# Residual and product blocks moved by DMA into the place of the low part, and transposed from there as fp32r

## What is computed

```python
# first block
h = rmsnorm(x, norm_attn);  q, k, v = split(h @ w_in)        # 8 dilated heads, 8 differential heads
x = x + concat(ya, yb) @ w_out                               # out_a, out_b
h = rmsnorm(x, norm_ffn)
x = x + (silu(h @ w_gate) * (h @ w_up)) @ w_down             # ffn1, inner width 5632
x = rmsnorm(x, norm_final)
# second block
z = rmsnorm(x) @ w_in2                                       # in_m, in_f, gate_m, gate_a
merged = g_a * (a_out @ w_proj_a) + g_m * (m_out @ w_proj_m) # proj_a ends this sum
x = x + merged @ w_out2                                      # out2
u = causal_dwconv(rmsnorm(x) @ w_up2)                        # ffn2
x = x + (silu(u_gate) * u_val) @ w_down2
```

## Time and profile before

| | us |
|---|---|
| median of 3 runs (2583.82 to 2584.75) | 2584.1 |
| profiled execution, its own time | 2584.64 |
| profiled execution, span of the instructions | 2582.8 |
| PE busy | 2562.9 (99% of the span) |
| weight loads of PE (beside its matmuls) | 2280.2 (88%) |
| DVE busy | 1453.2 (56%) |
| ACT busy | 1224.1 (47%) |
| DMA engines, mean busy share | 58%, 182 GB/s |

### The profile page before, as it was taken

One profiled execution on the slowest core, in us unless ns is written; L12 is line 12 of the kernel. 1 busy time (PEld: TensorE's weight loads), 2 busy tenths in 40 slices (PEclk: granted clock), 3 DMA queues, 4 the chain that ended last, 5 costly groups with the idle time before them and its releaser, 6 DMA issues.

```text
span 2582.8 us, 40276 instructions
## 1 busy us (share of the span) xinstructions
PE 2562.9 (99%) x14246; PEld 2280.2 (88%) x14246; DVE 1453.2 (56%) x1743; ACT 1224.1 (47%) x1677; POOL 104.4 (4%) x171
## 2 busy tenths in 40 slices
PE   8999999999999999999999999999999999999999
PEld 8999988888888888888899888788999899998997
DVE  5555555555555555555455545465576646765674
ACT  5665545444344434455455544544454434543443
POOL 1111100000000000000000000100000000000000
PEclk9999999999999999999999999999999999999999
DMA  7555556665665566666555655555555555555554
GB/s 214 155 159 162 168 183 186 189 188 192 193 191 187 189 194 191 191 196 188 166 168 170 187 170 172 163 171 185 176 181 184 195 189 185 181 188 194 173 191 165
DMA packets 328631, 469.37 MB, mean 182 GB/s; under 512 B 21911, under 2 KB 137810, under 8 KB 328402
## 3 DMA queue, kind: packets, MB, share of 16 engines
q1 hardware_dynamic: 328530, 468.04, 58.1%
HBM read 465.87 MB, written 2.10 MB: 181 GB/s over the span
## 4 chain that ended last, share of the span: by engine, by line
PE 84%; issue 14%; POOL 1%; SPq 0%; DMA 0%; DVE 0%; ACT 0%; POOLq 0%; DVEq 0%; ACTq 0%
PE ps L429 20%; PE ps L431 20%; PE ps L430 20%; PE ps L443 7%; PE ps L442 7%; PE ps L441 7%; PE ps L498 1%; PE ps L645 1%; PE ps L676 0%; PE ps L549 0%; POOL head_rstd L1844 0%; PE ps L480 0%; PE ps L486 0%; PE ps L568 0%; SPq L328 0%
## 5 line engine op out<-in xcount | busy, mean ns | idle before, releaser
L1276 DVE TENSOR_TENSOR w_lo<-raw,w_hi 128x1024 fp32r<-128x1024 f32 (+1 forms) x928 | 1095.3, 1185 | 1080.3 <-ACT w_hi L879 1079.0
L879 ACT ACTIVATE w_hi<-raw 128x1024 fp32r<-128x1024 f32 (+1 forms) x928 | 947.7, 1025 | 1151.0 <-PE ps L431 961.6
L429 PE MATMUL ps<-w_hi,xT_hi 128*128 128x512 f32 (+1 forms) x2400 | 906.8, 378 | 2.9 <-DVE w_lo L1276 2.8
L431 PE MATMUL ps<-w_hi,xT_lo 128*128 128x512 f32 (+1 forms) x2400 | 893.6, 372 | 0.0
L430 PE MATMUL ps<-w_lo,xT_hi 128*128 128x512 f32 (+1 forms) x2400 | 892.9, 372 | 0.0
L429 PEld LDWEIGHTS ps<-w_hi,xT_hi 128*128 128x128 f32 x2400 | 451.5, 188 | 69.4 <-issue 6.6
L431 PEld LDWEIGHTS ps<-w_hi,xT_lo 128*128 128x128 f32 x2400 | 451.1, 188 | 64.3
L430 PEld LDWEIGHTS ps<-w_lo,xT_hi 128*128 128x128 f32 x2400 | 451.7, 188 | 62.4
L441 PE MATMUL ps<-yT_hi,w_hi 128*128 128x256 f32 x1408 | 398.6, 283 | 0.0
L443 PE MATMUL ps<-yT_hi,w_lo 128*128 128x256 f32 x1408 | 398.5, 283 | 0.0
L442 PE MATMUL ps<-yT_lo,w_hi 128*128 128x256 f32 x1408 | 398.5, 283 | 0.0
(11 more groups left out here) (191 smaller groups left out, 994.4 us busy)
## 6 DMA issues: line engine op xcount, KB each, us to landing
raw<-in_w_up SPq DMA_DIRECT2D x264, 512.0 KB, 3.6
raw<-in_w_down SPq DMA_DIRECT2D x176, 512.0 KB, 4.4
raw<-in_w_in SPq DMA_DIRECT2D x112, 512.0 KB, 3.7
raw<-in_w_in SPq DMA_DIRECT2D x256, 192.0 KB, 2.6
raw<-in_w_gate SPq DMA_DIRECT2D x88, 512.0 KB, 3.5
raw<-in_w_out SPq DMA_DIRECT2D x60, 512.0 KB, 4.1
raw<-in_w_in SPq DMA_DIRECT2D x64, 384.0 KB, 3.3
raw<-in_w_proj_m SPq DMA_DIRECT2D x16, 512.0 KB, 3.5
```

The lines of the kernel that those rows point to most:

```text
L429: pe.matmul(o, hi[:, q], w_hi[n % NS][:, k, 0:width], start=first, stop=False)
L431: mm = pe.matmul(o, lo[:, q], w_hi[n % NS][:, k, 0:width], start=False, stop=last)
L879: nc.scalar.activation(w_hi[n % NS][:, :, 0:width], raw[n % NS][:, :, 0:width], ACT.Copy).then_inc(hi_ready, 1)
L1276: v.tensor_tensor(w_lo[n % NS][:, :, 0:width], raw[n % NS][:, :, 0:width], f32(w_hi[n % NS][:, :, 0:width]), ALU.subtract).then_inc(lo_rea ...
```

## The change

A semaphore and two steps come between DVE's result and PE's transposes. SP gets `move_x` and `move_act`: a DMA from `fresh` or `tok_act` to that part of `xT_lo` or `yT_lo` in which the low part of the same tiles will stand (ffn2's input is in `yT_lo`). A quarter of the residual goes in two DMAs of 256 KB, one for each tile of 128 tokens as soon as its addition is done, in rows of 256 words; the product goes in one DMA of 512 KB. The words are moved as they are, as float32. `turn_x` and `turn_act` now wait for the DMA (`x_moved`, `act_moved`), read from the destination, which has the type fp32r, and use an identity in fp32r (`ident_r`, one copy on ACT). They hang behind unit 2 instead of 1 (and `units + 2`), and so do `x_hi`, `x_lo` and, with them, `sum_squares`; `hi_part` and `lo_part` stay behind unit 2. To place the moves, SP's loops of the stages concerned are written out. `move_x` hangs behind the load of unit `(q + 1) * units + 7`, `move_act` behind that of unit 7 of the next block.

```diff
+        ident_r = sb("ident_r", [P], F32R)
...
+        def quarter(v, c0):
+            return v[:, c0:c0 + NT * W].rearrange("p (t n) -> p t n", t=NT)
...
+            def move_x(q, base, summed=None):
+
+                sem_, c0 = summed or (by_dve, FREE + SUMMED[base])
+                dst = (yT_lo if base == 4 * KT else xT_lo)[:, q * NT * W:(q + 1) * NT * W].bitcast(F32)
+                for t in range(NT):
+                    sp.wait_ge(sem_, c0 + 2 * q + t + 1)
+                    sp.dma_start(dst.rearrange("p (b t n) -> p b t n", b=2, t=NT)[:, :, t, :],
+                                 fresh[q % 2][:, t, :].rearrange("p (b n) -> p b n", b=2)).then_inc(x_moved[q % 2], 16)
+
+            def moving(units, base, summed=None):
+
+
+                def in_stage(u):
+                    for q in range(4):
+                        if u == (q + 1) * units + 7:
+                            move_x(q, base, summed)
+                return in_stage, lambda u: in_stage(4 * units + u)
+
+            def move_act(up, i):
+
+                sp.wait_ge(by_dve, at(i, FREE + PH[up][BY_DVE], 4))
+                dst = yT_lo[:, 12 * S:16 * S].bitcast(F32)
+                sp.dma_start(dst.rearrange("p (t n) -> p t n", t=NT), tok_act).then_inc(act_moved, 16)
...
+                if u > 16 and u % 16 == 7:
+                    move_act(f"ffn1_up{t}", u // 16)
...
-            def turn_x(q, base, summed=None):
-
-
-                sem_, c0 = summed or (by_dve, FREE + SUMMED[base])
-                pe.wait_ge(sem_, c0 + 2 * q + 2)
+            def turn_x(q, base):
+
+
+                pe.wait_ge(x_moved[q % 2], 32 * (2 * (base // KT - 1) + q // 2 + 1))
                 pe.wait_ge(kt_lo, base + 4 * q - 4)
+                moved = quarter(yT_lo if base == 4 * KT else xT_lo, q * NT * W).rearrange("p t n -> p (t n)")
+                moved = moved.rearrange("p (b t n) -> p b t n", b=2, t=NT)
                 for b in range(2):
                     for c in range(2):
                         for t in range(NT):
                             kt = 2 * b + c
-                            mm = pe.transpose(ps[4 + 2 * (q % 2) + b][:, c * S + t * P:c * S + (t + 1) * P],
-                                              fresh[q % 2][:, t, kt * P:(kt + 1) * P], ident[:])
+                            out_ = ps[4 + 2 * (q % 2) + b][:, c * S + t * P:c * S + (t + 1) * P]
+                            mm = pe.transpose(out_.bitcast(F32R), moved[:, b, t, c * P:(c + 1) * P], ident_r[:])
                     mm.then_inc(kt_T, 1)
...
-            def turn_act(up, fg, i):
-
-                pe.wait_ge(by_dve, at(i, FREE + PH[up][BY_DVE], 4))
+            def turn_act(fg, i):
+
+                pe.wait_ge(act_moved, at(i, 16 * (fg + 1), 16))
                 pe.wait_ge(tok_lo, at(i, FREE + 2 * fg, 2))
+                moved = quarter(yT_lo, 12 * S)
                 for f in range(4):
                     for t in range(NT):
-                        mm = pe.transpose(ps[4 + f // 2][:, f % 2 * S + t * P:f % 2 * S + (t + 1) * P],
-                                          tok_act[:, t, f * P:(f + 1) * P], ident[:])
+                        out_ = ps[4 + f // 2][:, f % 2 * S + t * P:f % 2 * S + (t + 1) * P]
+                        mm = pe.transpose(out_.bitcast(F32R), moved[:, t, f * P:(f + 1) * P], ident_r[:])
                 mm.then_inc(tok_T, 1)
...
             act.wait_ge(gain_ready, 3)
+            nc.scalar.activation(ident_r[:], ident[:], ACT.Copy).then_inc(warm, 1)
...
-                        if u == 1 and i == 1:
+                        if u == 2 and i == 1:
                             x_hi(1, base, dst, gain0)
-                        if u == units + 1:
+                        if u == units + 2:
                             x_hi(2 * i, base, dst, gain0)
```

More of the change, by code:

```diff
@@ L272, in two_blocks @@
         x2_ready, warm = sem("x2_ready"), sem("warm")
+        x_moved, act_moved = [sem(f"x_moved{j}") for j in range(2)], sem("act_moved")
         stored = sem("stored")
@@ L332, in heads_turn, with stream, turn @@
                             behind(8 * g + u)
-            def stream(name, loops, parts):
+            def stream(name, loops, parts, behind=None):
                 step = sum(len(units) for units, _, _ in parts)
-                with sp.Fori(0, loops) as i:
+                def turn(i, then=None):
                     n = PH[name][0]
@@ L344, in stream, with pairs @@
                             load(n, i, step, src, width)
+                            if then:
+                                then(n - PH[name][0])
                             n += 1
-            def pairs(name, loops, units, c0, width):
-                stream(name, loops, [(units, lambda i, g=g: i * (2 * width) + (c0 + g * width), width) for g in range(2)])
+                if behind:
+                    for i in range(loops):
+                        turn(i, lambda u, i=i: behind(i * step + u))
+                else:
+                    with sp.Fori(0, loops) as i:
+                        turn(i)
+            def pairs(name, loops, units, c0, width, behind=None):
+                stream(name, loops, [(units, lambda i, g=g: i * (2 * width) + (c0 + g * width), width) for g in range(2)], behind)
+            def move_x(q, base, summed=None):
[15 more added lines that the diff above has]
+                sp.dma_start(dst.rearrange("p (t n) -> p t n", t=NT), tok_act).then_inc(act_moved, 16)
             w_in, w_out, w_in2 = a["w_in"][0], a["w_out"][0], a["w_in_2"][0]
@@ L389, in _ @@
                         load(n, i, 8, src[:, :, c:c + W], W)
-            pairs("out_a", 2, rows(w_out, 0, HALF), 0, W)
+            own, after_out_a = moving(4, KT)
+            pairs("out_a", 2, rows(w_out, 0, HALF), 0, W, own)
             with nc.allow_non_contiguous_dma("a few gate columns"):
@@ L410, in _, with at_out2 @@
             pairs("gate_a", 2, rows(w_in2), OFF_GA, W)
-            pairs("proj_a", 2, rows(a["w_proj_a_2"][0]), 0, W)
-            pairs("out2", 2, rows(a["w_out_2"][0]), 0, W)
-            ffn("ffn2", a["w_up_2"][0], a["w_up_2"][0], FF, a["w_down_2"][0])
+            own, after_proj = moving(4, 3 * KT, (fresh_ready, 0))
+            pairs("proj_a", 2, rows(a["w_proj_a_2"][0]), 0, W, own)
+            own, after_out2 = moving(8, 4 * KT)
+            def at_out2(u):
+                after_proj(u)
+                own(u)
+            pairs("out2", 2, rows(a["w_out_2"][0]), 0, W, at_out2)
+            ffn("ffn2", a["w_up_2"][0], a["w_up_2"][0], FF, a["w_down_2"][0], lambda t, u: after_out2(u) if t == 0 else None)
             out_v = out[0].rearrange("(t p) n -> p t n", p=P)
@@ L644, in turn_x, with residual @@
                             kt = 2 * b + c
-                            mm = pe.transpose(ps[4 + 2 * (q % 2) + b][:, c * S + t * P:c * S + (t + 1) * P],
-                                              fresh[q % 2][:, t, kt * P:(kt + 1) * P], ident[:])
+                            out_ = ps[4 + 2 * (q % 2) + b][:, c * S + t * P:c * S + (t + 1) * P]
+                            mm = pe.transpose(out_.bitcast(F32R), moved[:, b, t, c * P:(c + 1) * P], ident_r[:])
                     mm.then_inc(kt_T, 1)
-            def residual(name, units, src, kt0, base, summed=None, last=None, ready=None, also=None, first=nothing):
+            def residual(name, units, src, kt0, base, last=None, ready=None, also=None, first=nothing):
                 for i in range(2):
@@ L830, in _ @@
             pe.wait_ge(by_act, FREE + PH["proj_a"][BY_ACT] - 2)
-            merge = 3 * KT, (fresh_ready, 0)
-            residual("proj_a", 4, yT, 0, *merge, ready=lambda u: pe.wait_ge(hf.y_lo, FREE + UK * (u + 1)),
+            residual("proj_a", 4, yT, 0, 3 * KT, ready=lambda u: pe.wait_ge(hf.y_lo, FREE + UK * (u + 1)),
                      also=(by_act, FREE + PH["proj_a"][BY_ACT]))
-            residual("out2", 8, xT, 0, 4 * KT, last=merge, ready=tiles_ready(3 * KT))
+            residual("out2", 8, xT, 0, 4 * KT, last=3 * KT, ready=tiles_ready(3 * KT))
             def broadcast_rstd():
```

66 lines of the change are left out of this document (38 added, 28 removed).

## The result

| | before | changed |
|---|---|---|
| median of 20 runs each, us | 2584.45 | 2588.06 |
| lowest and highest | 2583.82 to 2585.40 | 2585.66 to 2590.61 |
| span of the profiled execution | 2582.8 | 2586.4 |

The changed kernel is 3.6 us slower: ratio 1.0013, 95% interval 1.0007 to 1.0019. The loss is clear of the noise but under the 0.2% that the prediction took as its bound. It is not the 6.3 us gain that was forecast, and the median lies just outside the range (2571.5 to 2588.0).

What follows compares the result with a forecast made beforehand. PE's instruction stream was taken to bound the kernel. Batches gain 6.5 us and the place 0.9, together 7.4; less 1.1 for waits, 6.3 us less: from 2584.1 to 2577.8 us, range 2571.5 to 2588.

Steps and rivals of the forecast that it cites:

- The bound: Whole kernel: what PE issues is the time; a nanosecond off its stream shortens the kernel, a wait costs its full length.
- The transpose: PE's 27 batches of eight: an fp32r transpose takes 80 ns, against 111 ns for each present one.
- two cases of 67 and 107 ns: Pace of an fp32r transpose: 67 ns if loads are like transposes', weighed twice; 107 if like fp32r products'.
- the rival of a load bound: Batches on PE: loads bound transposes at 107 to 111 ns, only one place gains, 2584.3 us; chance 0.20.
- that of two passes: Batches on PE: fp32r at 128 columns no faster than two fp32 passes, 23 us more, 2606; chance 0.04.
- The term of 6.5 us for 26 batches: PE's batches except the one at ffn1's last down stage: each gains 0.25 us, 6.5 us together.
- The place: Last down stage of ffn1: the batch, now behind unit 2, uses PE's wait for the low part; 0.9 us gained.
- The waits: PE ahead of batches, for the DMA moves: 0.1 us for each of 11 products, none for 16 quarters, 1.1 us.
- The prediction's own sign of being wrong: Changed profile: batches still at 0.89 us, PE's waits for moves above 5 us in all, or a stage's first unit delayed.
- That fits, barely.: Residual quarter: the move lands by 396.0, PE reaches the batch at 396.2, 4.3 us after the second move's issue.
- The rival: Moves behind 512 KB of weights land after PE arrives; 2590 at 4.7 us landings, 2604 at 5.2; chance 0.13.
- What the prediction said of other queues: SP's queue: 43 moves carry 14 MB beside 469 MB, 3%; loads behind moves cost nothing, SP isn't waited for.

Runs made afterwards that it cites:

- the place alone: Kernel before, fp32 transposes from DVE's buffers, with batches, `x_hi`, `x_lo` and sums of squares hung one unit later; 2583.27 us, ratio 0.9996.
- the product at unit 3: Changed kernel with the products' transposes and high and low parts behind unit 3 instead of 2 in ten of eleven blocks; 2583.35 us, ratio 0.9997.
- with fp32: Changed kernel, its DMAs and places kept, but transposes read the moved words as plain fp32 with the fp32 identity; 2590.01 us, ratio 1.0023.
- early moves: Changed kernel with each move one place earlier in SP's order, ahead of the load that stood before it; 2579.39 us, ratio 0.9981.
- POOL's copies at the new place: POOL copies, typed fp32r on both sides, replace the changed kernel's DMAs; batches hang behind unit 2; 2579.52 us, ratio 0.9982.

## Why the prediction was wrong

**The bound was right.** PE's stream is the time: what was taken out of the batches or put ahead of them is in the medians, as the table shows.

**The transpose was sized right by luck, the batch was not.** The pace of fp32r transposes was taken as 80 ns, a weighted mean of two cases of 67 and 107 ns; it is 80 (0.64 us for eight). Neither case came, and nothing in the prediction's working leads to the value between them. The load record of a transpose is 141 ns, as for fp32:

```profile
L705 PEld LDWEIGHTS ps<-ident_r,xT_lo 128*128 128x128 f32 x96 | 9.1, 141 | 5.2 <-DMA xT_lo<-z 4.8
```

By the pace, the rival of a load bound (107 to 111 ns) and that of two passes (220 ns) fall. Of the Trainium skill's two rules, the 81 ns of "TensorE: Matmul & The Clock Gate", section "Back-to-back issue gap", agree with the trace; its "LDWEIGHTS" rule, 107 ns for 128 columns, does not hold as a lower bound for these. But the prediction set a batch at 0.64 against 0.89 and forgot that the 0.09 behind it (the matmul after the batch holds up its successor) would stay. It stays, at 0.07, so a batch costs 0.71 and the gain is 0.17 and not 0.25. The term of 6.5 us for 26 batches measures 4.4, or 4.6 for all 27.

**The place was right.** 0.9 us was said; 0.9 came in the trace and 1.3 in the median of the kernel with the place alone, and nothing was lost at the head of ffn2, in `x_lo` or in proj_a by the later place.

**The waits were the step that failed.** "I allow 0.1 us for each of 11, and nothing for the 16 quarters" made 1.1 us. Measured were 8.1 us idle and some 1.5 in longer batches, nearly all behind a wait. Forecast (-6.3) and result (+3.6) are 9.9 us apart. Of that the waits are 8.5 us, the short gain of the batches is 1.9, and the place gave 0.2 more; the three come to 10.2. The prediction's own sign of being wrong, waits above 5 us in all, came true. At the two places that were worked out the sum was nearly right: for the quarter 4.3 us from the second issue to PE and a landing of 4.1 were forecast, and 4.2 and 4.2 came (the second move of the earlier trace rows's place went out at 391.7, PE was there at 395.9); for the product 4.2 and 4.1 were forecast, and 4.2 and 4.3 came. What was wrong was to read "That fits, barely." as no cost. A margin of 0.1 or 0.2 us was carried over to 27 places whose landings spread by more: the median product lands after 4.5 us. The traces tell more: the four longest landings, 5.9, 5.5, 5.3 and 5.0 us, are all of moves whose load right ahead was itself late. Those four loads landed after 5.8, 5.6, 5.3 and 5.0 us, all others right ahead of a move after 3.5 to 4.4. The first stands behind the 1 MB gain, which could have been read from SP's order. Two of the four are loads of `w_down`, which land after 4.4 us in the median in the kernel before; the prediction used 3.6, the median of all loads, for every place. A smaller error of the same step: the issue of a quarter's move holds SP for 0.61 us or more, not 0.37.

**The rival decided.** Its words, "gone once they are late by 0.27 on average, a landing of 4.5 instead of 4.2 us", describe what happened, in place, in mechanism and nearly in size; with the true gain of 0.17 the point lies lower still, and the idle time is 0.30 a batch. It had a chance of 0.13, while the sum itself said that the margin was 0.2 us. A term that fits only just should have shared its chance about evenly with its rival.

**What the prediction said of other queues held.** The 43 moves carry 3% more bytes (the busy share of the DMA queue goes from 58 to 62%), and put ahead of the loads they made neither ACT nor PE wait longer for them.

The quarter at 1774.37 waited 1.05 us in the changed kernel's profiled execution, while with the product at unit 3 and with fp32 it hardly waited. Its moves landed after 4.0 and 5.3 us, and the load right ahead of them, at 1767.76, after 5.3; with the product at unit 3 that load took 4.2 us and the moves 4.0 and 4.3. Why such a load is late in one execution and not in another stays open. So does the wait of 0.80 and 0.99 us in those two kernels at a quarter of proj_a: with the product at unit 3 its second move landed after 3.9 us, though the load ahead was not late (3.5).

## What to carry to other kernels

- A small transfer that an engine waits for goes ahead of the bulk loads of its queue that have slack, not behind them: here one place in SP's order was worth 8.7 us, and no engine waited longer for a load.
- Compare the issue with the arrival at every place where a DMA replaces a direct read. If the margin is less than the spread of that queue's landings, count a wait and not a fit, and give the reader one unit more.
- The cost of a batch of another kind is taken up to the second matmul behind it; what the change of kind costs stays when the batch gets shorter.

## What the runs showed of the hardware

- **The same transfer, by what stands ahead.** 256 KB within SBUF, issued in pairs, landed 2.5 to 2.7 us after the issue when they went out ahead of the load (early moves, at 14 of 16 quarters; 4.2 and 4.6 at most at the other two), 2.7 to 3.0 when the pair began 1.8 us behind a load (changed kernel, proj_a), and 3.9 to 4.6 when it began 0.6 us behind a load of 512 KB (changed kernel, with 5.3 and 5.9 as exceptions). 512 KB within SBUF landed after 3.3 us in the median with early moves, and after 4.5 when issued 1.3 us behind a load (470.31 and 471.63 above).
- **The issue depends on the form.** A load's issue takes 0.37 us in the median in the changed kernel, and 0.59 right behind a move (472.21 in the kernel with early moves). A 512 KB move in rows of 512 words takes 0.47, a 256 KB move in rows of 256 words 0.61, though it carries half as much.
- **A batch behind a wait is 0.06 to 0.08 us longer** (0.71 against 0.64 in fp32r, 0.85 against 0.79 in fp32), besides the wait.
- **Times spread more where PE waits on DMAs.** The changed kernel's 20 runs lie within 4.95 us, the 20 of before within 1.6; with early moves 11 runs lie within 2.1, with POOL's copies at the new place within 1.6. That the waits are the cause is not shown.
- **POOL's copy and DVE's subtraction hold each other up.** From the kernel with the POOL copy at the new place, timeline of POOL and DVE at a product and at a quarter of proj_a:

```profile
471.28 1.04 POOL L1937 CAST yT_lo<-z 128x1024 fp32r<-128x1024 f32 x1 [33.66 <-DVE z L1551]
...
471.33 2.06 DVE L1335 TENSOR_TENSOR w_lo<-raw,w_hi 128x1024 fp32r<-128x1024 f32 x1
...
1705.59 1.97 POOL L1917 CAST xT_lo<-z 128x1024 fp32r<-128x1024 f32 x1 [33.02 <-DVE z L1746]
...
1705.44 1.22 DVE L1335 TENSOR_TENSOR w_lo<-raw,w_hi 128x1024 fp32r<-128x1024 f32 x1
```

Whichever starts first keeps its time (1.04 and 1.22), and the other takes about as much longer as the first still runs (2.06 for 1.22, 1.97 for 1.04). The Trainium skill's "SBUF — State Buffer", section "Who interferes with whom", says so of a DVE instruction with both inputs in SBUF and a GpSimd one that reads SBUF; the trace agrees. It is why the copies of proj_a took 1.97 us and not 1.04.
